# Up units of a squared-ReLU MLP as seven block products in place of eight

## The chip, the cores and the metric

The kernel runs on one core of a Trainium2 chip. The metric is the time of one execution in microseconds (us), as the device measures it. TensorE (PE) multiplies matrices into PSUM; VectorE (DVE), ScalarE (ACT) and GpSimd (POOL) work elementwise; SyncE (SP) issues transfers.

## What is computed

Two transformer blocks run one after the other on 512 tokens of 1024 features, in float32. The change touches the last piece of the second block:

```python
def sq_relu_mlp(h, w1, w2):
    return jnp.square(jax.nn.relu(h @ w1)) @ w2

    x = x + gt2[..., None, :] * sq_relu_mlp(modulate_2(rms_norm_2(x, norm2), sh2, sc2), w_mlp1, w_mlp2)
```

`w_mlp1` is 1024x4096 and `w_mlp2` is 4096x1024. Nothing else of the program is changed.

## The kernel before

**Data.** Features lie on the 128 partitions, tokens (T = 512) along the free axis; h is eight tiles of 128x512. Every float32 operand is split into a high part, rounded to the type fp32r, and the rest as a low part; `exact` and `products` multiply three times (high by high, high by low, low by high) and add up in PSUM.

**Units.** All weights come in units of 128x2048 floats (1 MB): 8 contraction tiles by 256 output features. A unit is loaded into `W_RAW[slot]` by SP, ScalarE casts it into `W_HI[slot]` (`split_hi`, L633), VectorE subtracts to get `W_LO[slot]` (`split_lo`, L1118), and TensorE does 8 tiles x 2 halves x 3 = 48 matmuls of 128x128 by 128x512 (L2059 to L2061). Slots alternate, so each unit is prepared while the one before it is multiplied. A unit fills two PSUM banks.

**The MLP.** It has four quarters, each of 4 up units and 4 out units: `quarter` at L571 (SP), L1086 (ACT), L1995 (DVE) and L2719 (PE). The first and the last are written out; the middle two are a hardware loop. For an up unit ScalarE applies ReLU to both banks (L1101), VectorE multiplies by the bank again, which is the square (L2010), casts to `G_HI` (L2020) and subtracts to `G_LO` (L2022). For an out unit VectorE adds both banks, gated, to the residual (`add_branch`, L1350).

**Order.** Each engine works its own queue in the order of the code. Semaphores order the engines: `landed` (a transfer), `hi_done` and `lo_done` (a unit split), `pe_done` (a unit multiplied), `evac_done` (its banks read), `relu_made`, `m_ready` (a tile of G ready for the out units). SP loads the next unit into a slot when the unit that held it has been split (`lo_done`).

Of the kernel before, what the change touches and what calls it, by code (L numbers as in the profile page):

```python
# [8 lines left out]
P = 128  # L9
# [177 lines left out]
def build(nc, ins, out):  # L187
    ctx_ = ExitStack()
    with ctx_:
        def sb(name, shape, dt=F32):  # L190
            return ctx_.enter_context(nc.sbuf_tensor(name, shape, dt))
# [133 lines left out]
        L_RAW = view("l_raw", 16, [P, KD, T])  # L325
        Y = view("merged", 0, [P, KD, T])
        SGB = [view(f"branch_gate{n}", 80 + 2 * n, [P, T]) for n in range(2)]
        STAT = sb("stat", [P, 64])

        PS = psum("ps", [P, 8 * T])  # L330
# [130 lines left out]
        def w_lo(u):  # L461


            return (W_RAW_LO if U_LR <= u.base < U_D + 2 else W_LO)[u.slot]

        block = ctx_.enter_context(nc.Block())

# [159 lines left out]
        def _(act):  # L627
# [455 lines left out]
            root(7)  # L1083
            h_hi(7, 7, U_MLP + 1)

            def quarter(q, last=False):  # L1086
                for j in range(4):
                    u = q.times(8) + (U_MLP + j)
                    if q.i is None and q.base == 0 and j == 0:
# [4 lines left out]
                    if not (q.i is None and q.base == 0 and j == 1):  # L1094
# [3 lines left out]
                    if q.i is None and q.base == 0 and j == 1:  # L1098
                        act.wait_ge(us_made, 3 * RAW.index(7) + 3)
                    for m in range(2):  # L1100
                        nc.scalar.activation(SA[m][:], BANK[2 * u.slot + m][:], ACT.Relu).then_inc(relu_made, 1)  # L1101
                for j in range(4):
                    if not (last and j == 3):
                        split_hi(q.times(8) + (U_MLP + 5 + j))

            quarter(at(0))
            with act.Fori(0, 2) as i:
                quarter(At(1, i, 1))
            quarter(at(3), True)
# [3 lines left out]
        def _(dve):  # L1113
# [878 lines left out]
            each(dve, 4, 0, 2, out_pair)  # L1992
            norm_split(7, 7, U_MLP + 1, (6, 7))

            def quarter(q, last_one=False):  # L1995
                for j in range(4):
                    u = q.times(8) + (U_MLP + j)
                    first = q.i is None and q.base == 0 and j == 0
                    if first:
                        raw_out(7)  # L2000
                    elif not (q.i is None and q.base == 0 and j == 1):
                        split_lo(u + 1)
                    for m in range(2):
                        t = 2 * j + m
                        n = q.times(8) + (t + 1)
                        dve.wait_ge(relu_made, n.v)
                        if first:
# [3 lines left out]
                        if first and m == 1:  # L2011
                            mul.then_inc(us_made, 1)
                            dve.wait_ge(us_made, 3 * RAW.index(7) + 3)
                        elif m == 1:
                            mul.then_inc(evac_done, 1)
                            dve.wait_ge(evac_done, (u + 1).v)
                        else:
                            mul.then_inc(y_a, 1)
                            dve.wait_ge(y_a, (q.times(4) + (KD + j + 1)).v)
                        nc.vector.tensor_copy(G_HI[:, t, :], GT[m][:]).then_inc(m_hi_made, 1)  # L2020
                        dve.wait_ge(m_hi_made, n.v)
                        nc.vector.tensor_tensor(G_LO[:, t, :], GT[m][:], G_HI[:, t, :].bitcast(F32), ALU.subtract).then_inc(m_ready, 1)  # L2022
                for j in range(4):
                    u = q.times(8) + (U_MLP + 4 + j)
                    if not (last_one and j == 3):
                        split_lo(u + 1)
                    dve.wait_ge(pe_done, (u + 1).v)
                    for m in range(2):
                        if last_one and j == 3 and m == 1:
                            last.then_inc(evac_done, 1)  # L2030
                            dve.wait_ge(pe_done, N_UNITS + 1)
                        last = add_branch(at(2 * j + m), BANK[2 * u.slot + m], 7)
                    last.then_inc(evac_done, 1)

            quarter(at(0))
            with dve.Fori(0, 2) as i:
                quarter(At(1, i, 1))
            quarter(at(3), True)
# [3 lines left out]
        def _(pe):  # L2042
# [676 lines left out]
            def quarter(q, count=4):  # L2719
                first = q.i is None and q.base == 0  # L2720
                for j in range(1 if first else 0, 4):
                    ready = (lambda k: pe.wait_ge(h_ready, H_BASE[7] + k + 1)) if first and j == 1 else None
                    products(q.times(8) + (U_MLP + j), KD, 2, h_part(H_HI), h_part(H_LO), ready).then_inc(pe_done, 1)
# [4 lines left out]
            quarter(at(0))  # L2728
            with pe.Fori(0, 2) as i:
                quarter(At(1, i, 1))  # L2730
            quarter(at(3), 3)
# [5 lines left out]
def weight_units(inputs):  # L2737


    w = {n: np.asarray(inputs[n]) for n in ("ffn_w_in", "ffn_w_out", "pool_w", "conv_w_in", "conv_w_out", "w_in_2",  # L2740
                                            "w_br_attn_2", "w_br_gla_2", "w_out_2", "w_mlp1_2", "w_mlp2_2")}
    units = np.zeros((N_UNITS, P, FULL), np.float32)

    def put(u, a, *cols):

        rows = np.concatenate([a[:, c:c + n].reshape(-1, P, n) for c, n in cols], axis=2).transpose(1, 0, 2)
        units[u, :, :rows[0].size] = rows.reshape(P, -1)

    for f in range(4):
        w_in, w_out = w["ffn_w_in"][f // 2, f % 2], w["ffn_w_out"][f // 2, f % 2]  # L2750
        for half in range(2):
            base = U_FFN[f] + half * (IN_UNITS + OUT_UNITS)
            for j in range(IN_UNITS):
                c = (half * FH + j) * P
                put(base + j, w_in, (c, P), (F + c, P))
            for m in range(OUT_UNITS):
                put(base + IN_UNITS + m, w_out[half * FH * P:(half + 1) * FH * P], (m * P, P))
    put(U_POOL, w["pool_w"][0].reshape(-1, 2 * P), (0, 2 * P))
    for j in range(8):
        put(U_CONV + j, w["conv_w_in"][0], (D + j * P, P), (2 * D + j * P, P))  # L2760
# [67 lines left out]
```

## Time and profile before

| | us |
|---|---|
| median of 3 runs | 2727.92 |
| lowest and highest | 2725.42, 2728.01 |
| the profiled execution | 2728.2 |
| its span, first to last instruction | 2726.1 |
| TensorE busy in the span | 2697.3 (99%) |
| VectorE busy | 1582.7 (58%) |
| ScalarE busy | 851.3 (31%) |

The mean granted TensorE clock is 0.997 of full speed. The span is 2.1 us shorter than the execution's own time. In the rows further down, a busy time of an instruction runs from its start to its end; two instructions of one engine can overlap by a little, so the distance from start to start is what an engine's queue costs.

### The profile page before, as it was taken

Reading aid. Unit: us, or ns where it says so; the run is one execution under the profiler, and the core shown is the slowest. Engines: PE = TensorE matmul, PEld = TensorE weight load, DVE = VectorE, ACT = ScalarE, POOL = GpSimd, SP = SyncE. Lnnn points to the kernel's source line nnn. Section 1 sums busy time; section 2 is a strip of 40 time slices with the busy share of each in tenths; the row PEclk is TensorE's granted clock in tenths of the full one; section 3 lists DMA queues with packets and bytes.
Section 4 is the critical chain, followed back from the end, with each engine's and each line's share of the span. In section 5 each row is a group of like instructions: output and inputs, shape, how many; then the busy total and the mean of one; then the engine's idle time right before and its main releaser. Section 6 shows DMA issues by size and latency. Waiting matters only on the chain.

```text
span 2726.1 us, 32568 instructions
## 1 busy us (share of the span) xinstructions
PE 2697.3 (99%) x12826; PEld 2255.3 (83%) x12826; DVE 1582.7 (58%) x2168; ACT 851.3 (31%) x956; POOL 74.2 (3%) x148
## 2 busy tenths in 40 slices
PE   7999999999999999999999999999999999999999
PEld 4888888888888888888888888899898888888887
DVE  6644658635576358554764445777687632654434
ACT  4212234222242122331421333345545512432221
POOL 0000000000001000000010000000000000000000
PEclk9999999999999999999999999999999999999999
DMA  7644523625526346222263332202212332222222
GB/s 289 233 144 168 203 100 124 226 106 187 180 103 240 130 156 223 100 100 101 92 243 119 131 109 95 102 36 68 69 53 66 128 135 92 93 93 94 94 106 77
DMA packets 61860, 355.05 MB, mean 130 GB/s; under 512 B 7104, under 2 KB 8896, under 8 KB 31680
## 3 DMA queue, kind: packets, MB, share of 16 engines
q1 hardware_dynamic: 42208, 252.20, 25.7%
q0 software_dynamic: 19120, 100.70, 10.5%
q8 instruction: 70, 1.15, 0.2%
q10 hardware_dynamic: 432, 0.75, 0.1%
q14 instruction: 30, 0.25, 0.0%
HBM read 343.66 MB, written 7.86 MB: 129 GB/s over the span
## 4 chain that ended last, share of the span: by engine, by line
PE 95%; DVE 3%; ACT 1%; issue 0%; DMA 0%; DVEq 0%; ACTq 0%
PE ps L2059 24%; PE ps L2060 24%; PE ps L2061 24%; PE ps L2279 5%; PE ps L2281 5%; PE ps L2280 5%; PE ps L2534 2%; PE ps L2479 1%; PE ps L2528 1%; PE ps L2079 1%; PE ps L2081 1%; PE ps L2080 1%; DVE h_lo L1257 0%; DVE w_lo L1118 0%; PE ps L2449 0%
## 5 line engine op out<-in xcount | busy, mean ns | idle before, releaser
L2059 PE MATMUL ps<-h_hi,w_hi 128*128 128x512 f32 x1888 | 736.4, 390 | 6.4 <-DVE g_t L1337 3.3
L2060 PE MATMUL ps<-h_lo,w_hi 128*128 128x512 f32 x1888 | 735.2, 389 | 0.0
L2061 PE MATMUL ps<-h_hi,w_lo 128*128 128x512 f32 x1888 | 735.1, 389 | 0.0
L633 ACT CAST w_hi<-w_raw 128x2048 fp32r<-128x2048 f32 (+1 forms) x238 | 419.3, 1762 | 598.6 <-PE ps L2061 517.9
L1118 DVE TENSOR_TENSOR w_lo<-w_raw,w_hi 128x2048 fp32r<-128x2048 f32 (+1 forms) x214 | 447.6, 2092 | 118.3 <-ACT w_hi L633 118.1
L2059 PEld LDWEIGHTS ps<-h_hi,w_hi 128*128 128x128 f32 x1888 | 354.7, 188 | 82.0 <-DVE g_t L1337 3.0
L2061 PEld LDWEIGHTS ps<-h_hi,w_lo 128*128 128x128 f32 x1888 | 354.9, 188 | 74.0
L2060 PEld LDWEIGHTS ps<-h_lo,w_hi 128*128 128x128 f32 x1888 | 354.9, 188 | 73.3
L2059 PE MATMUL ps<-g_hi,w_hi 128*128 128x512 f32 x944 | 367.3, 389 | 0.0
L2061 PE MATMUL ps<-g_hi,w_lo 128*128 128x512 f32 x944 | 367.2, 389 | 0.0
L2060 PE MATMUL ps<-g_lo,w_hi 128*128 128x512 f32 x944 | 367.2, 389 | 0.0
L1350 DVE SCALAR_TENSOR_TENSOR x_res<-ps,gate,x_res 128x512 f32<-128x512 f32 x120 | 87.6, 749 | 343.7 <-PE ps L2061 334.8
L722 ACT ACTIVATE silu_a<-ps 128x512 f32<-128x512 f32 x85 | 50.9, 599 | 638.9 <-PE ps L2061 633.8
L1373 DVE TENSOR_TENSOR g_t<-silu_a,ps 128x512 f32<-128x512 f32 x85 | 58.4, 687 | 301.4 <-ACT silu_a L722 301.4
L1133 DVE SCALAR_TENSOR_TENSOR ada<-ada,cond 128x1024 f32<-128x1024 f32 x176 | 207.9, 1220 | 1.6 <-DMA ada<-in_ada_t 1.5
L2061 PEld LDWEIGHTS ps<-g_hi,w_lo 128*128 128x128 f32 x944 | 177.2, 188 | 36.8
L2059 PEld LDWEIGHTS ps<-g_hi,w_hi 128*128 128x128 f32 x944 | 177.2, 188 | 36.7
L2060 PEld LDWEIGHTS ps<-g_lo,w_hi 128*128 128x128 f32 x944 | 177.2, 188 | 36.6
L2279 PE MATMUL ps<-h_hi,w_hi 128*128 128x512 f32 (+3 forms) x304 | 120.1, 395 | 0.5 <-DVE h_lo L1257 0.5
L2281 PE MATMUL ps<-h_hi,w_raw_lo 128*128 128x512 f32 (+3 forms) x304 | 113.5, 373 | 0.0
L2280 PE MATMUL ps<-h_lo,w_hi 128*128 128x512 f32 (+3 forms) x304 | 113.2, 372 | 0.0
L602 POOL DMA_DIRECT2D ada<-in_ada_t x64 | 33.8, 528 | 1359.2 <-DVE ada L1133 1356.6
(370 smaller groups left out, 3020.9 us busy)
## 6 DMA issues: line engine op xcount, KB each, us to landing
w_raw<-in_units SPq DMA_DIRECT2D x175, 1024.0 KB, 4.8
ada<-in_ada_t POOLq DMA_DIRECT2D x56, 1024.0 KB, 7.1
w_raw<-in_units SPq DMA_DIRECT2D x64, 704.0 KB, 4.0
ada<-in_ada_t POOLq DMA_DIRECT2D x64, 512.0 KB, 4.8
ada_first<-in_ada_t SPq DMA_DIRECT2D x8, 1024.0 KB, 12.1
x_res<-in_x SPq DMA_DIRECT2D x4, 512.0 KB, 7.8
x_home<-x_res POOLq DMA_DIRECT2D x1, 2048.0 KB, 8.3
attn_tq<-attn_qx SPq DMA_DIRECT2D x32, 64.0 KB, 2.0
```

Source lines behind the costliest of these rows:

```text
L633: nc.scalar.copy(W_HI[u.slot][:, 0:n], W_RAW[u.slot][:, 0:n]).then_inc(hi_done, 1)
L1118: nc.vector.tensor_tensor(w_lo(u)[:, 0:n], W_RAW[u.slot][:, 0:n], W_HI[u.slot][:, 0:n].bitcast(F32), ALU.subtract).then_inc(lo_done, 1)
L1133: return nc.vector.scalar_tensor_tensor(tile, tile, 1.0, COND[cond][:], ALU.mult, ALU.mult, accum_out=MOD_SUMS[:, bass.ds(n.v, 1)])
L1350: return nc.vector.scalar_tensor_tensor(x, bank[:], GATE[:, bass.ds((m + 8 * gate).v, 1)], x, ALU.mult, ALU.add)
L1373: nc.vector.tensor_tensor(GT[u.slot][:], SA[u.slot][:], bank[:], ALU.mult).then_inc(evac_done, 1)
L2059: pe.matmul(dst, hi[:, k, c], rhs_hi(k), start=(k == 0), stop=False)
L2060: pe.matmul(dst, hi[:, k, c], rhs_lo(k), start=False, stop=False)
L2061: last = pe.matmul(dst, lo[:, k, c], rhs_hi(k), start=False, stop=(k == kt - 1))
L2279: pe.matmul(dst, a_hi, b_hi, start=first, stop=False)
L2280: pe.matmul(dst, a_hi, b_lo, start=False, stop=False)
L2281: return pe.matmul(dst, a_lo, b_hi, start=False, stop=last)
L2534: last = pe.matmul(BANK[7][:, 2 * P:4 * P], VA[:, t, HD * (i // 2):HD * (i // 2 + 1)], PT[:, t, :, :].rearrange("p n q -> p (n q)"), start ...
```

## The change

The twelve up units of quarters 1 to 3 are computed by Strassen's product in Winograd's form. The 256 output features of a unit, its 1024 inputs and the 512 tokens are each halved, and the product is made from seven products of block sums in place of eight block products. In detail:

- The weights of such a unit lie in four quarters of 128x512 in DRAM (`put_quarters`). VectorE forms four sums of them (`w_sum_1` to `w_sum_4`); the seven left operands ("forms" 0 to 6) are three raw quarters, the third sum, which takes the place of a quarter, and three sum tiles. ScalarE casts each form to its high part and VectorE subtracts, form by form. Forms have fixed places in `W_HI` and `W_LO`, so form f of the next unit can be cast once product f of this unit is done.
- Once, during the out units of quarter 0, the block sums of h are made (`h_forms`, `h_forms_hi`): for each of 4 tiles six sums on VectorE, one cast on ScalarE, one 128x1024 subtraction on VectorE. They stay for all twelve units.
- TensorE does 7 products x 4 tiles x 3 = 84 matmuls of 128x128 by 128x256 a unit, into four banks, of which 256 columns each are used. Products 0 and 4 go to bank a, 2 and 5 to bank d, 3 and 6 to bank c, 1 to b. So product 4 waits for a copy of product 0 (`P_1`, ScalarE), product 5 for VectorE's second mixing step and product 6 for its third.
- VectorE puts the output together in seven additions of 128x256 (`mix` 0 to 5) into the SBUF tiles `C_1` and `C_2`. ScalarE does ReLU, the square and the cast to `G_HI` of each 128x512 tile (`squared`), and VectorE makes the eight `G_LO` tiles in the fourth up unit (`m_lo`).
- Quarter 0 and all out units keep their matmuls. The forms of a quarter's first up unit are made in the out unit before it.

The core of the diff, without 8 leading spaces (left out: semaphore names, tiles, `h_forms`, the renamed loops of quarter 0, `put_quarters`, and the deleted general `quarter`):

```diff
+def form_at(w, f):
+    return w[S0 if f < 4 else 1 - S0][:, (f % 4) * 4 * P:(f % 4 + 1) * 4 * P]
+def form_src(v, f):
+    return (raw_quarter(v, 0), S_2[:], raw_quarter(v, 2), S_1[:], raw_quarter(v, 1), raw_quarter(v, 3), S_4[:])[f]
+SUM_OF = {1: 3, 2: 2, 3: 1, 6: 4}
+def four(j):
+    return [BANK[4 * (j % 2) + n][:, 0:TC] for n in range(4)]
...
+    def form_hi_split(v, s, f, first=False):
+        if f == 0:
+            act.wait_ge(landed[v.slot], (v + 1).half().times(16).v)
+        elif f in SUM_OF:
+            act.wait_ge(sum_made, (s.times(4) + (SUM_MADE + SUM_OF[f])).v)
+        if first:
+            if f == 0:
+                act.wait_ge(pe_done, (v - 1).v)
+            if f == 4:
+                act.wait_ge(pe_done, v.v)
+        elif f < 6:
+            act.wait_ge(form_mm, (s.times(6) + (FORM_MM - 6 + f + 1)).v)
+        else:
+            act.wait_ge(pe_done, v.v)
+        nc.scalar.copy(form_at(W_HI, f), form_src(v, f)).then_inc(form_hi if f < 6 else hi_done, 1)
+    def whole_hi(v, s):
+        act.wait_ge(landed[v.slot], (v + 1).half().times(16).v)
+        for n in range(2):
+            act.wait_ge(form_mm, (s.times(6) + (FORM_MM + 2 * n + 2)).v)
+            c = slice(n * FULL // 2, (n + 1) * FULL // 2)
+            half = nc.scalar.copy(W_HI[v.slot][:, c], W_RAW[v.slot][:, c])
+        half.then_inc(hi_done, 1)
+    def squared(q, s, m, tile):
+        act.wait_ge(m_sq_made, (s.times(2) + (M_SQ + m - 1)).v)
+        nc.scalar.activation(SA[m][:], (C_2, C_1)[m][:], ACT.Relu).then_inc(relu_made, 1)
+        act.wait_ge(relu_made, (s.times(2) + (RELUS + m + 1)).v)
+        nc.scalar.activation(M_SQUARE[:, tile, :], SA[m][:], ACT.Square).then_inc(m_sq_made, 1)
+        act.wait_ge(m_sq_made, (s.times(2) + (M_SQ + m + 1)).v)
+        nc.scalar.copy(G_HI[:, tile, :], M_SQUARE[:, tile, :]).then_inc(m_hi_act, 1)
+    def mixed_unit(q, j):
+        u, s = q.times(8) + (U_MLP + j), sums_unit(q, j)
+        act.wait_ge(form_mm, (s.times(6) + (FORM_MM + 1)).v)
+        act.wait_ge(mix_made, (s.times(6) + (MIX_MADE - 1)).v)
+        nc.scalar.copy(P_1[:], four(j)[0]).then_inc(p1_made, 1)
+        if j < 3:
+            for f in range(6):
+                form_hi_split(u + 1, s + 1, f)
+        else:
+            whole_hi(u + 1, s)
+        act.wait_ge(mix_made, (s.times(6) + (MIX_MADE + 6)).v)
+        squared(q, s, 0, 2 * j)
+        if j < 3:
+            form_hi_split(u + 1, s + 1, 6)
+        act.wait_ge(evac_done, (u + 1).v)
+        squared(q, s, 1, 2 * j + 1)
...
+    def w_sum_1(v, s):
+        dve.wait_ge(landed[v.slot], (v + 1).half().times(16).v)
+        dve.wait_ge(form_lo, (s.times(6) + (FORM_LO - 2)).v)
+        nc.vector.tensor_tensor(S_1[:], raw_quarter(v, 2), raw_quarter(v, 3), ALU.add).then_inc(sum_made, 1)
+    def w_sum_3(v, s):
+        dve.wait_ge(sum_made, (s.times(4) + (SUM_MADE + 1)).v)
+        nc.vector.tensor_tensor(raw_quarter(v, 2), raw_quarter(v, 0), raw_quarter(v, 2), ALU.subtract).then_inc(sum_made, 1)
+    def w_sum_2(v, s):
+        dve.wait_ge(sum_made, (s.times(4) + (SUM_MADE + 1)).v)
+        nc.vector.tensor_tensor(S_2[:], S_1[:], raw_quarter(v, 0), ALU.subtract).then_inc(sum_made, 1)
+    def w_sum_4(v, s):
+        dve.wait_ge(sum_made, (s.times(4) + (SUM_MADE + 3)).v)
+        dve.wait_ge(lo_done, v.v)
+        nc.vector.tensor_tensor(S_4[:], raw_quarter(v, 1), S_2[:], ALU.subtract).then_inc(sum_made, 1)
+    def form_lo_split(v, s, f):
+        if f < 6:
+            dve.wait_ge(form_hi, (s.times(6) + (FORM_HI + f + 1)).v)
+        else:
+            dve.wait_ge(hi_done, (v + 1).v)
+        nc.vector.tensor_tensor(form_at(W_LO, f), form_src(v, f), form_at(W_HI, f).bitcast(F32),
+                                ALU.subtract).then_inc(form_lo if f < 6 else lo_done, 1)
+    def mix(q, j, n):
+        u, s = q.times(8) + (U_MLP + j), sums_unit(q, j)
+        a, b, d, c = four(j)
+        add = lambda out, x, bank: nc.vector.tensor_tensor(out, x, bank, ALU.add)
+        mixed = lambda n: dve.wait_ge(mix_made, (s.times(6) + (MIX_MADE + n)).v)
+        product = lambda f: dve.wait_ge(form_mm, (s.times(6) + (FORM_MM + f + 1)).v)
+        if n == 0:
+            dve.wait_ge(p1_made, (s + (P1_MADE + 1)).v)
+            mixed(0)
+            product(1)
+            add(U_2[:], P_1[:], b).then_inc(mix_made, 1)
+        if n == 1:
+            product(2)
+            mixed(1)
+            add(U_3[:], U_2[:], d).then_inc(mix_made, 1)
+        if n == 2:
+            product(3)
+            mixed(2)
+            dve.wait_ge(relu_made, (s.times(2) + (RELUS - 1)).v)
+            add(C_2[:, TC:T], U_3[:], c).then_inc(mix_made, 1)
+            dve.wait_ge(evac_done, u.v)
+            add(U_4[:], U_2[:], c).then_inc(mix_made, 1)
+        if n == 3:
+            product(4)
+            dve.wait_ge(relu_made, (s.times(2) + RELUS).v)
+            add(C_1[:, 0:TC], P_1[:], a).then_inc(mix_made, 1)
+        if n == 4:
+            product(5)
+            add(C_2[:, 0:TC], U_3[:], d).then_inc(mix_made, 1)
+        if n == 5:
+            dve.wait_ge(pe_done, (u + 1).v)
+            mixed(4)
+            add(C_1[:, TC:T], U_4[:], c).then_inc(evac_done, 1)
+    def m_lo(q, tile):
+        dve.wait_ge(m_hi_act, (q.times(8) + (M_HI_ACT - 8 + tile + 1)).v)
+        nc.vector.tensor_tensor(G_LO[:, tile, :], M_SQUARE[:, tile, :], G_HI[:, tile, :].bitcast(F32), ALU.subtract).then_inc(m_ready, 1)
+    def mixed_unit(q, j):
+        v, t = q.times(8) + (U_MLP + j + 1), sums_unit(q, j + 1)
+        if j == 3:
+            mix(q, j, 0)
+            mix(q, j, 1)
+            m_lo(q, 0)
+            m_lo(q, 1)
+            mix(q, j, 2)
+            m_lo(q, 2)
+            m_lo(q, 3)
+            split_lo(v)
+            mix(q, j, 3)
+            mix(q, j, 4)
+            m_lo(q, 4)
+            m_lo(q, 5)
+            mix(q, j, 5)
+            m_lo(q, 6)
+            m_lo(q, 7)
+            return
+        w_sum_1(v, t)
+        form_lo_split(v, t, 0)
+        w_sum_3(v, t)
+        w_sum_2(v, t)
+        mix(q, j, 0)
+        w_sum_4(v, t)
+        mix(q, j, 1)
+        form_lo_split(v, t, 1)
+        mix(q, j, 2)
+        form_lo_split(v, t, 2)
+        form_lo_split(v, t, 3)
+        mix(q, j, 3)
+        form_lo_split(v, t, 4)
+        mix(q, j, 4)
+        form_lo_split(v, t, 5)
+        mix(q, j, 5)
+        form_lo_split(v, t, 6)
...
+            elif not last_one:
+                if first:
+                    dve.wait_ge(t_ready, T_READY + 4)
+                w_sum_1(u + 1, q.times(4))
+                w_sum_3(u + 1, q.times(4))
+                w_sum_2(u + 1, q.times(4))
+                w_sum_4(u + 1, q.times(4))
+                for f in range(4):
+                    form_lo_split(u + 1, q.times(4), f)
...
+    def mixed_unit(q, j):
+        u, s = q.times(8) + (U_MLP + j), sums_unit(q, j)
+        a, b, d, c = four(j)
+        tokens = lambda hi, lo, k0, t0: lambda k: (hi[:, k0 + k, t0:t0 + TC], lo[:, k0 + k, t0:t0 + TC])
+        form = lambda n: lambda k: (T_HI[:, k, n * TC:(n + 1) * TC], T_LO[k // 2][:, k % 2, n * TC:(n + 1) * TC])
+        for f, dst, x in ((0, a, tokens(H_HI, H_LO, 0, 0)),
+                                 (1, b, form(1)),
+                                 (2, d, form(2)),
+                                 (3, c, form(0)),
+                                 (4, a, tokens(H_HI, H_LO, 4, 0)),
+                                 (5, d, form(3)),
+                                 (6, c, tokens(H_HI, H_LO, 4, TC))):
+            if f < 6:
+                pe.wait_ge(form_lo, (s.times(6) + (FORM_LO + f + 1)).v)
+            else:
+                pe.wait_ge(lo_done, (u + 1).v)
+            if f == 0:
+                pe.wait_ge(evac_done, (u - 1).v)
+            if f == 1:
+                pe.wait_ge(t_ready, T_READY + 4)
+            if f == 2 and j == 0:
+                pe.wait_ge(evac_done, u.v)
+            if f == 4:
+                pe.wait_ge(p1_made, (s + (P1_MADE + 1)).v)
+            if f == 5:
+                pe.wait_ge(mix_made, (s.times(6) + (MIX_MADE + 2)).v)
+            if f == 6:
+                pe.wait_ge(mix_made, (s.times(6) + (MIX_MADE + 4)).v)
+            hi, lo = form_at(W_HI, f), form_at(W_LO, f)
+            for k in range(4):
+                x_hi, x_lo = x(k)
+                cc = slice(k * P, (k + 1) * P)
+                last = exact(dst, hi[:, cc], lo[:, cc], x_hi, x_lo, k == 0, k == 3)
+            last.then_inc(form_mm if f < 6 else pe_done, 1)
```

## Rows read from the trace of the kernel before

**Rows 1.** The page, part 1 (busy time by engine) and part 4 (chain).

```profile
PE 2697.3 (99%) x12826; PEld 2255.3 (83%) x12826; DVE 1582.7 (58%) x2168; ACT 851.3 (31%) x956; POOL 74.2 (3%) x148
...
PE 95%; DVE 3%; ACT 1%; issue 0%; DMA 0%; DVEq 0%; ACTq 0%
```

**Rows 2.** Busy PE, PEld, DVE, ACT, POOL; PEclk; DMA share, GB/s: quarter 2, up, out.

```profile
2548.80:2592.30 43.50, 43.50 (x194) 36.03 (x193) 20.88 (x24) 10.58 (x10) 0.00 (x0) 1.00 0.26 96
2592.30:2635.80 43.50, 43.50 (x194) 36.03 (x193) 16.84 (x16) 8.63 (x6) 0.00 (x0) 1.00 0.28 97
```

**Rows 3.** TensorE in order of time: start, us, engine; 128x512 stream, 63 steps apart.

```profile
2500.40 0.39 PE L2059 MATMUL ps<-h_hi,w_hi 128*128 128x512 f32 x1
...
2514.68 0.39 PE L2059 MATMUL ps<-g_hi,w_hi 128*128 128x512 f32 x1
```

**Rows 4.** TensorE in order of time, 128x256 stream, 42 steps apart.

```profile
1738.40 0.28 PE L2279 MATMUL ps<-w_hi,h_hi 128*128 128x256 f32 x1
...
1743.44 0.28 PE L2279 MATMUL ps<-w_hi,h_hi 128*128 128x256 f32 x1
```

**Rows 5.** VectorE by line and shape: count | busy us, mean ns | idle before.

```profile
L1118 DVE TENSOR_TENSOR w_lo<-w_raw,w_hi 128x2048 fp32r<-128x2048 f32 x151 | 345.4, 2287 | 85.5 <-ACT w_hi L633 85.3 <-DVE conv_out L1546 0.2
```

**Rows 6.** VectorE in order of time, four places.

```profile
1720.14 0.42 DVE L1611 TENSOR_TENSOR low_rank<-ps,low_rank 32x256 fp32r<-32x256 f32 x1
1720.48 0.67 DVE L1613 TENSOR_TENSOR low_rank<-ps,low_rank 32x512 fp32r<-32x512 f32 x1
...
2172.16 4.90 DVE L1948 TENSOR_TENSOR l_lo<-l_raw,l_hi 128x512 fp32r<-128x512 f32 x8
...
2548.88 1.41 DVE L1350 SCALAR_TENSOR_TENSOR x_res<-ps,gate,x_res 128x512 f32<-128x512 f32 x2 [6.64 <-PE ps L2061]
...
2560.39 0.69 DVE L2010 TENSOR_TENSOR g_t<-silu_a,ps 128x512 f32<-128x512 f32 x1 [7.27 <-ACT silu_a L1101]
2561.11 0.43 DVE L2020 CAST g_hi<-g_t 128x512 fp32r<-128x512 f32 x1
```

**Rows 7.** ScalarE in order of time, three places.

```profile
23.26 0.72 ACT L770 ACTIVATE g_t<-g_t,mods 128x512 f32<-128x512 f32 x1 [4.49 <-DVE g_t L1449]
24.02 0.62 ACT L772 CAST h_hi<-g_t 128x512 fp32r<-128x512 f32 x1
...
2169.82 4.26 ACT L1053 CAST l_hi<-l_raw 128x512 fp32r<-128x512 f32 x8
...
2559.76 1.09 ACT L1101 ACTIVATE silu_a<-ps 128x512 f32<-128x512 f32 x2 [8.96 <-PE ps L2061]
2560.73 1.92 ACT L633 CAST w_hi<-w_raw 128x2048 fp32r<-128x2048 f32 x1
```

**Rows 8.** ScalarE by line and shape.

```profile
L646 ACT ACTIVATE g_t<-x_res 128x512 f32<-128x512 f32 x56 | 34.4, 624 | 52.9 <-DVE x_res L1350 29.3 <-DVE ssq L1186 14.4 <-DVE ssq L1190 9.2
...
L856 ACT CAST low_rank<-ps 96x256 fp32r<-96x256 f32 x1 | 0.4, 368 | 3.3 <-PE ps L2281 3.3
```

**Rows 9.** In order of time: VectorE ends, TensorE restarts.

```profile
2395.44 0.68 DVE L1337 TENSOR_TENSOR g_t<-ps,ssq 128x512 f32<-128x512 f32 x1
...
2396.27 0.47 PE L2059 MATMUL ps<-h_hi,w_hi 128*128 128x512 f32 x1 [1.12 <-DVE g_t L1337]
2396.58 0.40 PE L2060 MATMUL ps<-h_lo,w_hi 128*128 128x512 f32 x1
```

**Rows 10.** As rows 2, for two stretches; and two starts 12 steps apart.

```profile
1698.00:1700.00 2.00, 2.00 (x10) 2.00 (x11) 0.79 (x4) 0.21 (x1) 0.00 (x0) 0.50 0.04 8
...
2394.00:2396.00 2.00, 1.15 (x6) 0.61 (x4) 2.00 (x4) 0.00 (x0) 0.00 (x0) 1.00 0.00 0
...
1699.05 0.41 PE L2280 MATMUL ps<-h_lo,w_hi 128*128 128x256 f32 x1
...
1701.61 0.41 PE L2280 MATMUL ps<-h_lo,w_hi 128*128 128x256 f32 x1
```

**Rows 11.** The page, part 6: weight transfers, KB each, us to landing.

```profile
w_raw<-in_units SPq DMA_DIRECT2D x175, 1024.0 KB, 4.8
```

More of the change, by code:

```diff
@@ new lines, in outs, with first_quarter @@
+            def outs(q, last=False, first=False):
+                for j in range(4):
+                    if j < 3:
+                        split_hi(q.times(8) + (U_MLP + 5 + j))
+                    elif not last:
+                        for f in range(7):
+                            form_hi_split(q.times(8) + (U_MLP + 8), q.times(4), f, True)
+                    if first:
+                        for kk in ((0,), (1, 2), (3,), ())[j]:
+                            h_forms_hi(kk)
+            def first_quarter():
+                for j in range(4):
+                    u = at(U_MLP + j)
+                    if j == 0:
@@ L1093, in quarter @@
                         continue
-                    if not (q.i is None and q.base == 0 and j == 1):
+                    if j > 1:
                         split_hi(u + 1)
@@ L1101, in quarter @@
                         nc.scalar.activation(SA[m][:], BANK[2 * u.slot + m][:], ACT.Relu).then_inc(relu_made, 1)
+                outs(at(0), first=True)
+            def quarter(q, last=False):
                 for j in range(4):
-                    if not (last and j == 3):
-                        split_hi(q.times(8) + (U_MLP + 5 + j))
-            quarter(at(0))
+                    mixed_unit(q, j)
+                outs(q, last)
+            first_quarter()
             with act.Fori(0, 2) as i:
@@ L2000, in quarter, with first_quarter @@
+            def first_quarter():
+                for j in range(4):
+                    u = at(U_MLP + j)
+                    if j == 0:
                         raw_out(7)
-                    elif not (q.i is None and q.base == 0 and j == 1):
+                    elif j > 1:
                         split_lo(u + 1)
@@ L2018, in quarter @@
                             mul.then_inc(y_a, 1)
-                            dve.wait_ge(y_a, (q.times(4) + (KD + j + 1)).v)
+                            dve.wait_ge(y_a, KD + j + 1)
                         nc.vector.tensor_copy(G_HI[:, t, :], GT[m][:]).then_inc(m_hi_made, 1)
-                        dve.wait_ge(m_hi_made, n.v)
+                        dve.wait_ge(m_hi_made, t + 1)
                         nc.vector.tensor_tensor(G_LO[:, t, :], GT[m][:], G_HI[:, t, :].bitcast(F32), ALU.subtract).then_inc(m_ready, 1)
+                outs(at(0), first=True)
+            def quarter(q, last_one=False):
                 for j in range(4):
[L2024 to L2035, printed above, removed]
+                    mixed_unit(q, j)
+                outs(q, last_one)
+            first_quarter()
             with dve.Fori(0, 2) as i:
@@ L2717, in last_unit @@
                     last.then_inc(pe_done, 1)
[L2719 to L2723, printed above, removed]
+            def mixed_unit(q, j):
[12 more added lines that the diff above has]
+                        pe.wait_ge(form_lo, (s.times(6) + (FORM_LO + f + 1)).v)
+                    else:
+                        pe.wait_ge(lo_done, (u + 1).v)
[17 more added lines that the diff above has]
+                    last.then_inc(form_mm if f < 6 else pe_done, 1)
@@ L2747, in put, with put_quarters @@
         units[u, :, :rows[0].size] = rows.reshape(P, -1)
+    def put_quarters(u, a, *cols):
+        blocks = [a[4 * P * half:4 * P * (half + 1), c:c + P].reshape(4, P, P).transpose(1, 0, 2).reshape(P, 4 * P)
+                  for c in cols for half in range(2)]
+        units[u] = np.concatenate(blocks, axis=1)
     for f in range(4):
```

102 lines of the change are left out of this document (89 added, 13 removed).

## The prediction

> **What bounds the kernel now.** I read the busy times first [rows 1]: TensorE is busy 99% of the span and carries 95% of the chain that ended last, VectorE is busy 58%, ScalarE 31%. Then the stretches of one quarter of the MLP [rows 2]: TensorE is busy all of the 43.5 us of its up units and all of its out units, VectorE 20.9 and 16.8 us, ScalarE 10.6 and 8.6. So here nothing but TensorE's stream counts. Its pace has to be taken from starts, not from durations, since a matmul of 0.39 us overlaps the next: 63 steps in 14.28 us are 0.2267 us for 512 columns [rows 3], 48 of them 10.88 us a unit. A stream of 256 columns is in the trace too: 42 steps in 5.04 us, 0.120 us each [rows 4], each with a weight load of its own, as in the new code.
>
> **TensorE's share of the change.** 84 x 0.120 = 10.08 us in place of 10.88: 0.80 us less for each of twelve units, 9.6 us at most. It is less than an eighth, because 256 columns cost 0.53 of 512.
>
> The Trainium skill, in "TensorE: Matmul & The Clock Gate" (Back-to-back issue gap), has isolated matmuls start every N / 2.4 + 2.5 ns; by that a unit would go from 10.36 to 9.17 us and the most to be had would be 14 us. The trace has 0.2267 and 0.120 where the rule gives 0.216 and 0.109, so the rows decide.
>
> **What the other two engines get.** Prices from start to start. VectorE: a 128x512 subtraction 0.60 (8 in 4.90, the last one lasting 0.69), 128x256 0.34, the next instruction when it needs the result of the one before 0.03 after its end [rows 6]; the two additions to the residual 1.32 together [rows 6]; a whole split 2.29 [rows 5]. ScalarE: a 128x512 cast from SBUF 0.52 (8 in 4.26), lasting 0.62, the next dependent one 0.04 after the end [rows 7]; the square of 128x512 lasts 0.62 as well, and the 256 columns from PSUM 0.37, so 0.28 in a queue [rows 8]. From ScalarE's end to VectorE's start 0.03 [rows 6, 7].
>
> For one of the first three up units VectorE has 4 sums and 7 subtractions of 512 columns and 7 additions of 256: 11 x 0.60 + 7 x 0.34 = 9.0 us. ScalarE has 7 casts, 6 steps of `squared` and the copy of product 0: about 8.1 us with the dependent steps. Both fit into 10.08 taken alone. They don't fit together, because the two queues wait for each other in a ring that closes once a unit:
>
> - ScalarE, from the end of `mix` 4 (both halves of `C_2`): handover 0.04, ReLU 0.66, square 0.66, cast 0.52, the cast of form 6 0.52, the second `squared` 1.83, `P_1` 0.28, the cast of form 0 for the unit after next 0.62 and 0.03: 5.15 us.
> - VectorE, from there: the subtraction of form 0 stands near the front of the next unit's queue, and behind it come `w_sum_3`, `w_sum_2`, `mix` 0, `w_sum_4`, `mix` 1, form 1, `mix` 2 (two), forms 2 and 3, `mix` 3, form 4, `mix` 4: 8 x 0.60 + 5 x 0.34 + 0.43 = 6.93 us.
>
> Sum 12.08 us a turn, whatever TensorE does. TensorE hangs on it at product 5, which needs `mix` 1 (bank d read); `mix` 1 ends 3.77 us before `mix` 4.
>
> **A quarter, clock at TensorE's first product of its first up unit.** Forms 0 to 3 are ready.
>
> Unit 0: VectorE does the residual additions from 0.20 to 1.52, forms 4 to 6 to 3.33, then its queue without a pause, `mix` 1 ending at 7.1, before product 5 is due (7.20), and `mix` 4 at 10.86. No stall; the unit ends at 10.08.
>
> Unit 1: one turn on, `mix` 4 ends at 22.94 and `mix` 1 at 19.17. Product 5 was due at 17.28. TensorE restarts 0.15 after VectorE's end and its first step is 0.08 longer than 0.23 [rows 9]: 19.40, a stall of 2.1 us. Products 5 and 6 take 2.88: 22.28.
>
> Unit 2: `mix` 1 ends at 31.25, product 5 starts at 31.48 where 29.48 was due: 2.0 us. Unit end 34.36.
>
> Unit 3: VectorE has no forms to make. `P_1` is copied at 39.24, `mix` 1 ends at 40.5, product 5 is due at 41.5: no stall; end 44.44. But VectorE's queue goes on with `m_lo` 0 and 1 (1.2), `mix` 2 (0.68), `m_lo` 2 and 3 (1.2), and only then the split of the first out unit, 43.5 to 45.8. The out unit starts at 46.0: a stall of 1.6 us.
>
> Out units: 4 x 10.88 to 89.55, where 8 x 10.88 = 87.04 stood before. Their VectorE work (four sums, seven subtractions, 6.6 us more in the last) fits beside 16.8 of 43.5 us [rows 2].
>
> So 3.2 us gained and 5.7 lost: 2.5 us more a quarter, 7.5 in three. From the profiled execution's 2728.2 that is 2735.7; its time and the median of 2727.9 differ by 0.3, and I forecast 2736.
>
> **The rest.** The sums of h in quarter 0 cost VectorE about 5.3 us a tile (two additions and a cast waited for, four of 256 columns, 1.2 for the subtraction, half a split's price): 21 us, with its other work some 41 of the 43.5 us of out units. The crowded place is the second out unit, 14 us of work in 10.88; the banks it reads late are wanted one unit on, and by my queue VectorE catches up 2.6 us before the quarter ends. Cost nothing; if that cover is gone, the overrun. Weight transfers are as many and land after 4.8 us [rows 11]; a unit is issued when its slot's forms are split, 4 us into a unit at worst, and wanted no sooner than a unit later. SP and GpSimd queues are untouched otherwise. ReLU from SBUF isn't in the trace: between 0.60 and the 0.72 of an activation with a bias [rows 7, 8]; I take the square's 0.62. Up to four such steps lie in a turn, so -0.1 to +0.4 us. The new code waits more, often two or three times before a 0.34 us addition, on values worked out in the loop. ScalarE passes two such waits without a gap within 0.47 us [rows 7], so one costs between nothing and 0.24 us, hidden as long as the instruction before is running. Unseen, I take nothing; behind blocking waits it could add up to 1 us a turn.
>
> **Rivals.**
>
> *TensorE stays the bound.* If ScalarE and VectorE overlapped better than the queue order allows, each unit would take 10.08: 2728.2 - 9.6 = 2718.6. It decides if the turn is under 10.1 us, 2 us less than my sum. For it: both engines' plain sums are under 10.08. Against: every price in the ring is a row. 0.07.
>
> *The ring holds, the closing stall doesn't.* If the split in unit 3 came 1.6 us earlier, a quarter would cost +0.9: 2731, within what can be told from no change. 0.13.
>
> *Waits lengthen the ring.* With 1 us more a turn, units 1 and 2 and what follows shift: 2 to 2.5 us a quarter, 2742 to 2743; with two, 2749. 0.17.
>
> *The clock falls.* At 1698 to 1700 the granted clock was 0.50, half of 2.4 GHz, after a run of one-column products, and a 256-column step took 0.213 us (12 in 2.56) [rows 10]; at 2394 to 2396, with a gap of 1.1 us, it stayed at 1.00. My stalls are 2 us, longer than any in these rows. Four microseconds at the half clock lose 1.8; after the first two stalls the ring hides it, ahead of the out units about 0.3 to 2.2 a quarter isn't: 2737 to 2742, I take 2740. 0.05. The Trainium skill, in "TensorE: Matmul & The Clock Gate" (What's actually happening), gates the clock to half after an idle window; by that rule this rival would win only if a stall grows beyond those I expect, and no row shows a 2 us gap.
>
> *It doesn't do what it says,* 256-column steps paced by the weight load (0.19): excluded by rows 4.
>
> **How the numbers follow.** My forecast has 0.58, own range 2731 to 2741. A measurement of this kernel tells about 0.2% (5.5 us) from no change, so "slower" begins at 2733.4. Faster 0.08 (first rival, rounded up); same 0.18 (second rival, and 0.05 of mine); slower 0.74. The range takes in the second rival and most of the third and fourth: 2729 to 2746.
>
> **What would show it.** In the profile after: 256-column steps of 0.120; in quarters 1 to 3 up units of 10.1, 12.1, 12.1 and 10.1 us, with TensorE idle about 2 us before product 5, put down to VectorE's `mix` 1; the first out unit waiting 1.6 us for `w_lo`; VectorE waiting for the cast of form 0, ScalarE for `mix` 4; clock 1.00. Units 1 and 2 of 10.1 us make the ring wrong; 13 us and more, or gaps before each short addition, the cost of waits; a stall in quarter 0, the cover for the sums of h.

## The result, and the profile after

The changed kernel takes 2735.69 us, median of 6 runs (2732.01 to 2736.21), beside 2727.76 us (6 runs, 2723.74 to 2728.15) for the kernel before: a ratio of 1.0029, 95% interval 1.0016 to 1.0042. On a second chip (10 and 15 runs) it was 2732.9 beside 2725.38, 1.0026 (1.0017 to 1.0035). So it is slower by 7.5 to 7.9 us, though TensorE has less to do. The forecast was 2736, slower by 7.5.

The page of the changed kernel, part 1, where [rows 1] had 2697.3 us on TensorE, 1582.7 on VectorE and 851.3 on ScalarE. The profiled execution took 2732.01 us, its span 2730.2:

```profile
PE 2690.3 (99%) x13258; PEld 2269.0 (83%) x13258; DVE 1654.6 (61%) x2352; ACT 914.3 (33%) x1095; POOL 74.3 (3%) x148
```

TensorE is busy 7 us less in a span that is 4 us longer. Now one quarter, the third as in [rows 2], split where its first out unit starts (from, to; us; busy PE, PEld, DVE, ACT, POOL; granted clock; DMA share, GB/s):

```profile
2547.60:2593.60 46.00, 41.02 (x337) 40.41 (x335) 36.71 (x69) 27.18 (x48) 0.00 (x0) 1.00 0.26 91
2593.60:2637.10 43.50, 43.47 (x192) 36.02 (x193) 19.58 (x24) 11.61 (x13) 0.00 (x0) 1.00 0.27 96
```

The up units take 46.0 us in place of 43.5 and TensorE idles 5 of them, at full clock. VectorE has 36.7 us of work in 46 and ScalarE 27.2: neither is full. TensorE in order of time shows where it idles (start, us, engine, line; in brackets the idle time and who ended it):

```profile
2547.59 0.28 PE L2550 MATMUL ps<-h_hi,w_hi 128*128 128x256 f32 x1
...
2564.84 0.28 PE L2552 MATMUL ps<-h_hi,w_lo 128*128 128x256 f32 x1
2566.97 0.36 PE L2550 MATMUL ps<-h_forms_hi,w_hi 128*128 128x256 f32 x1 [1.85 <-DVE mix L2171]
...
2577.00 0.28 PE L2552 MATMUL ps<-h_hi,w_lo 128*128 128x256 f32 x1
2579.04 0.36 PE L2550 MATMUL ps<-h_forms_hi,w_hi 128*128 128x256 f32 x1 [1.76 <-DVE mix L2171]
...
2591.95 0.28 PE L2552 MATMUL ps<-h_hi,w_lo 128*128 128x256 f32 x1
2593.63 0.49 PE L2330 MATMUL ps<-g_hi,w_hi 128*128 128x512 f32 x1 [1.40 <-DVE w_lo L1238]
...
2637.28 0.28 PE L2550 MATMUL ps<-h_hi,w_hi 128*128 128x256 f32 x1
```

Three gaps and no other: before product 5 of units 1 and 2, waiting for `mix`, and ahead of the first out unit, waiting for the split of its weights. In the quarter's own clock product 5 starts at 19.38 and 31.45, the out unit at 46.04, the next quarter at 89.69.

The ring, one turn of it. First ScalarE, then VectorE, in order of time:

```profile
2558.52 0.63 ACT L1168 ACTIVATE silu_a<-mixed 128x512 f32<-128x512 f32 x1 [1.38 <-DVE mixed L2171]
...
2560.90 0.63 ACT L1168 ACTIVATE silu_a<-mixed 128x512 f32<-128x512 f32 x1
...
2562.75 0.36 ACT L1179 COPY prod<-ps 128x256 f32<-128x256 f32 x1
2563.01 0.62 ACT L1149 CAST w_hi<-w_raw 128x512 fp32r<-128x512 f32 x1
...
2570.59 0.63 ACT L1168 ACTIVATE silu_a<-mixed 128x512 f32<-128x512 f32 x1 [1.29 <-DVE mixed L2171]
```

```profile
2557.99 0.41 DVE L2171 TENSOR_TENSOR mixed<-mix,ps 128x256 f32<-128x256 f32 x1
...
2561.02 0.69 DVE L2164 TENSOR_TENSOR w_lo<-w_sum,w_hi 128x512 fp32r<-128x512 f32 x1 [1.68 <-ACT w_hi L1149]
2561.63 0.69 DVE L2143 TENSOR_TENSOR w_sum<-w_raw 128x512 f32<-128x512 f32 x1
2563.67 0.69 DVE L2164 TENSOR_TENSOR w_lo<-w_raw,w_hi 128x512 fp32r<-128x512 f32 x1 [1.35 <-ACT w_hi L1149]
...
2566.41 0.41 DVE L2171 TENSOR_TENSOR mix<-mix,ps 128x256 f32<-128x256 f32 x1
...
2570.15 0.41 DVE L2171 TENSOR_TENSOR mixed<-mix,ps 128x256 f32<-128x256 f32 x1
```

`mix` 4 at 2557.99 lets ScalarE begin the squares of unit 0. The cast of form 0 stands behind both squares and `P_1` in ScalarE's queue and starts at 2563.01. VectorE waits for it 1.35 us, goes on without a pause from 2563.67, and reaches `mix` 1 (which frees product 5) at 2566.41 and the next `mix` 4 at 2570.15. Then ScalarE is released again. A turn is 12.16 us; TensorE's unit is 10.08.

All waits from the first of these quarters to the end, summed (us in total, times, longest), four of them:

```profile
ACT silu_a L1168 <- DVE mixed L2171: 25.1, 12, 5.1
DVE w_lo L2164 <- ACT w_hi L1149: 21.6, 15, 1.7
...
PE ps L2550 <- DVE mix L2171: 9.3, 6, 1.9
...
PE ps L2330 <- DVE w_lo L1238: 2.7, 2, 1.4
```

Six waits for `mix`, so the ring is there in every quarter, and two for the split: in the first of the three quarters a lower clock had slowed TensorE just before (see the last section), and of that stall 0.39 us from start to start was left, too little to be listed. From here on a "quarter" is the time from one first product to the next; for the last one, where no quarter follows, it is the time to the span's end less the 3.39 us that the kernel before has there (90.43 - 87.04, spans unrounded). The changed kernel has 89.89, 89.69 and 89.54 where 87.04 stood, 8.0 us together.

### The profile page after: what moved, and what is told of

The parts are those of the page before. It is cut to its first block and busy times, and to the rows that moved or that the text cites. A ratio compares the mean times of both kernels' runs of the same rounds, so it can differ in the third digit from the quotient of the medians.

```text
span 2730.2 us, 34144 instructions
## 1 busy us (share of the span) xinstructions
PE 2690.3 (99%) x13258; PEld 2269.0 (83%) x13258; DVE 1654.6 (61%) x2352; ACT 914.3 (33%) x1095; POOL 74.3 (3%) x148
## 5 line engine op out<-in xcount | busy, mean ns | idle before, releaser
L2330 PE MATMUL ps<-h_hi,w_hi 128*128 128x512 f32 x1696 | 661.7, 390 | 6.4 <-DVE g_t L1457 3.3
L2331 PE MATMUL ps<-h_lo,w_hi 128*128 128x512 f32 x1696 | 660.4, 389 | 0.0
L2332 PE MATMUL ps<-h_hi,w_lo 128*128 128x512 f32 x1696 | 660.4, 389 | 0.0
L681 ACT CAST w_hi<-w_raw 128x2048 fp32r<-128x2048 f32 (+1 forms) x223 | 390.6, 1751 | 520.4 <-PE ps L2332 438.7
L2330 PEld LDWEIGHTS ps<-h_hi,w_hi 128*128 128x128 f32 x1696 | 318.8, 188 | 74.4 <-DVE g_t L1457 3.0
L2332 PEld LDWEIGHTS ps<-h_hi,w_lo 128*128 128x128 f32 x1696 | 318.8, 188 | 66.3
L2331 PEld LDWEIGHTS ps<-h_lo,w_hi 128*128 128x128 f32 x1696 | 318.8, 188 | 66.0
L2332 PEld LDWEIGHTS ps<-g_hi,w_lo 128*128 128x128 f32 x944 | 177.2, 188 | 36.7
L2550 PE MATMUL ps<-h_hi,w_hi 128*128 128x512 f32 (+3 forms) x448 | 161.1, 360 | 0.5 <-DVE h_lo L1377 0.5
L2551 PE MATMUL ps<-h_lo,w_hi 128*128 128x512 f32 (+3 forms) x448 | 154.3, 344 | 0.0
L2550 PEld LDWEIGHTS ps<-h_hi,w_hi 128*128 128x128 f32 (+1 forms) x448 | 85.8, 191 | 12.7 <-issue 1.4
```

The lines of the kernel that those rows point to most:

```text
L681: nc.scalar.copy(W_HI[u.slot][:, 0:n], W_RAW[u.slot][:, 0:n]).then_inc(hi_done, 1)
L2330: pe.matmul(dst, hi[:, k, c], rhs_hi(k), start=(k == 0), stop=False)
L2331: pe.matmul(dst, hi[:, k, c], rhs_lo(k), start=False, stop=False)
L2332: last = pe.matmul(dst, lo[:, k, c], rhs_hi(k), start=False, stop=(k == kt - 1))
L2550: pe.matmul(dst, a_hi, b_hi, start=first, stop=False)
L2551: pe.matmul(dst, a_hi, b_lo, start=False, stop=False)
```

## Experiments

Each edit is shown against the changed kernel. The theory is the ring: what matters is only what stands between `mix` 4 and the cast of form 0 on ScalarE, and VectorE's queue from there. The rivals are that ScalarE or VectorE is simply short of time (the sum of its work), and that short instructions with several waits cost something of their own.

**The split sooner.** VectorE, in the last up unit, splits the out unit's weights ahead of the four subtractions for the squares.

```diff
-                    m_lo(q, 0)
-                    m_lo(q, 1)
                     mix(q, j, 2)
-                    m_lo(q, 2)
-                    m_lo(q, 3)
                     split_lo(v)
+                    for tile in range(4):
+                        m_lo(q, tile)
```

> One part of the VectorE order moved: in the fourth up unit of a quarter the split of the first out unit stands right behind mix 2 (and mix 2 ahead of the m_lo tiles), not behind four m_lo. Theory (the stall at the head of the out units is the queue position of the split): the split ends at about 43.7 of the quarter's clock, before TensorE is through with the unit at 44.4, so that stall (1.4 to 1.6 us) is gone, 3 to 5 us in three quarters: 2731 to 2733 against 2735.7. The two stalls ahead of product 5 stay at 2 us each. Rival (VectorE has too much work in the up units, wherever it stands): no change.

Measured: 2730.14 us (10 runs) beside 2724.81 (20 runs), 1.0019 (1.0009 to 1.0028). Two quarters of 88.20, where 89.69 stood. In the second of them the two gaps before product 5 stay at 2.13 and 2.05 from start to start; in the first the clock fell after the first gap, and the second one shrank to 0.56. The closing gap is gone, on TensorE:

```profile
2591.38 0.28 PE L2550 MATMUL ps<-h_hi,w_lo 128*128 128x256 f32 x1
2591.57 0.50 PE L2328 MATMUL ps<-g_hi,w_hi 128*128 128x512 f32 x1
```

So the closing stall is VectorE's queue order, worth 1.5 us a quarter, and independent of the ring. The last quarter, though, took 89.50; why is told below, with the clock. That leaves 3.2 us for the three quarters in the trace. The times alone hardly show it: 1.0019 stands beside 1.0026 and 1.0029, and the intervals overlap.

**The squares late.** ScalarE alone is reordered: the squares of unit u are made in unit u+1, the first behind the cast of form 0, the second behind that of form 3. The work is the same.

```diff
                 nc.scalar.copy(P_1[:], four(j)[0]).then_inc(p1_made, 1)
-                if j < 3:
-                    for f in range(6):
+                    form_hi_split(u + 1, s + 1, 0)
+                if j > 0:
+                    square_of(j - 1, 0)
+                if j < 3:
+                    for f in range(1, 4):
                         form_hi_split(u + 1, s + 1, f)
...
-                squared(q, s, 0, 2 * j)
+                if j > 0:
+                    square_of(j - 1, 1)
                 if j < 3:
-                    form_hi_split(u + 1, s + 1, 6)
-                act.wait_ge(evac_done, (u + 1).v)
-                squared(q, s, 1, 2 * j + 1)
+                    for f in range(4, 7):
+                        form_hi_split(u + 1, s + 1, f)
+                else:
+                    square_of(3, 0)
+                    square_of(3, 1)
```

> Only ScalarE's order changed: the two squares of an up unit are made in the unit after it, the first behind the cast of form 0, the second behind the cast of form 3. Same instructions on every engine. Theory (a ring of ScalarE and VectorE through mix 4, the squares, P_1 and form 0): the ring is opened, VectorE's 9.0 us and ScalarE's 8.1 us a unit fit under TensorE's 10.08, the stalls ahead of product 5 go, at most 0.3 us is left at the head of the out units: a quarter of 84.1 us in place of 89.8, 17 us less in three, 2719. Rival (one of the two engines is full): no change, or under 2 us.

Measured: 2716.11 us (5 runs) beside 2724.81, 0.9968 (0.9954 to 0.9982), 0.3% faster than the kernel before. Quarters 84.35, 84.33 and 84.25. No gap before product 5 is left; ScalarE, in the unit that had the ring:

```profile
2554.50 0.62 ACT L1149 CAST w_hi<-w_raw 128x512 fp32r<-128x512 f32 x1
2555.02 0.63 ACT L1168 ACTIVATE silu_a<-mixed 128x512 f32<-128x512 f32 x1
```

The cast of form 0 now stands ahead of the ReLU, and the ReLU no longer waits, since its `mixed` is long made. The same instructions on the same engines, in another order, are worth 5.4 us a quarter. That excludes both sums of work as the cause of the loss, and the waits themselves, which are all still there.

**Only the second square late.** The second square of a unit is made behind `P_1` and the cast of form 0 of the next unit; the first stays.

```diff
+                def second(jj):
+                    act.wait_ge(evac_done, (q.times(8) + (U_MLP + jj + 1)).v)
+                    squared(q, sums_unit(q, jj), 1, 2 * jj + 1)
+
                 if j < 3:
-                    for f in range(6):
+                    form_hi_split(u + 1, s + 1, 0)
+                if j > 0:
+                    second(j - 1)
+                if j < 3:
+                    for f in range(1, 6):
                         form_hi_split(u + 1, s + 1, f)
...
-                act.wait_ge(evac_done, (u + 1).v)
-                squared(q, s, 1, 2 * j + 1)
+                else:
+                    second(3)
```

> Only the second square of a unit moves, behind P_1 and the cast of form 0 of the next unit. Theory: the ring gets shorter by exactly the 1.83 us of one square, 12.1 to 10.3 us a turn, so the stalls ahead of product 5 fall from 2.0 to 0.2 or 0.3 us, not to zero; with about 0.5 us left at the head of the out units a quarter takes 84.8 us, 2721. Rival (stalls come from another wait that the order of the squares touches only by the way): stalls that aren't 1.8 us shorter.

Measured: 2722.01 us (8 runs) beside 2724.81, 0.9986 (0.9975 to 0.9996); quarters 85.51, 85.51 and 85.35. The direction holds, the size does not: 0.7 us above what was expected. VectorE shows why:

```profile
2554.99 0.41 DVE L2180 TENSOR_TENSOR mixed<-mix,ps 128x256 f32<-128x256 f32 x1
...
2558.02 0.69 DVE L2173 TENSOR_TENSOR w_lo<-w_sum,w_hi 128x512 fp32r<-128x512 f32 x1 [1.68 <-ACT w_hi L1149]
...
2565.70 0.41 DVE L2180 TENSOR_TENSOR mixed<-mix,ps 128x256 f32<-128x256 f32 x1
```

A second ring lay under the first. It closes through the cast of form 6, which still stands behind the first square: 2.62 us from `mix` 4's end to VectorE's start on form 6, then 8.09 us of VectorE to the next `mix` 4, its queue now with form 6, `w_sum_1` and form 0 ahead. Sum 10.71 (product 5 starts 10.62 apart, at 2562.54 and 2573.16), still above 10.08, and 1.45 below the first ring rather than the 1.83 that the square takes.

**Each square twice.** ScalarE takes the square of every tile twice, first into a tile that nobody reads.

```diff
+                nc.scalar.activation(GT[m][:], SA[m][:], ACT.Square)
                 nc.scalar.activation(M_SQUARE[:, tile, :], SA[m][:], ACT.Square).then_inc(m_sq_made, 1)
```

> The order of the changed kernel, but ScalarE makes each square twice, once into an unused tile: 0.53 us more for each of two tiles a unit. ScalarE's sum goes from 8.1 to 9.2 us, still under TensorE's 10.08. Theory: the work lies in the ring, 12.1 to 13.2 us a turn, and adds up over the three turns of a quarter: about 3.2 us a quarter, 9.5 in all, 2745. Rival (only the sum of an engine's work counts): no change.

Measured: 2741.59 us (4 runs) beside 2724.81, 1.0058 (1.0041 to 1.0075); quarters 92.83, 92.83 and 92.67, 2.9 to 3.1 above the changed kernel. Product 5 now starts every 13.11 us (2478.60, 2491.71) where 12.07 stood: 1.04 more, and two squares of 0.54 from start to start are 1.08. The gap, on TensorE:

```profile
2569.03 0.28 PE L2553 MATMUL ps<-h_hi,w_lo 128*128 128x256 f32 x1
2571.43 0.35 PE L2551 MATMUL ps<-h_forms_hi,w_hi 128*128 128x256 f32 x1 [2.12 <-DVE mix L2172]
```

What ScalarE gets in the ring comes out at the end, nearly one for one. A second, smaller gap is new: product 4 starts 0.80 after the matmul before it (at 2567.62), since `P_1` now comes late as well; it lies within the 13.11.

**The changed kernel again,** on the chip of the next two.

> The changed kernel once more, on the same chip as the two that follow, so that they stand against it as well as against the kernel before. Every theory expects quarters of 89.7 to 89.9 us on TensorE's clock and a time 7.5 to 8 us above the kernel before: 2732 to 2736, ratio 1.003.

Measured: 2732.9 us (10 runs) beside 2725.38 (15 runs); quarters 89.87, 89.70 and 89.54.

**Squares late and split sooner.** Both edits together.

> Two edits together: ScalarE makes the squares of unit u in unit u+1, behind the first and the third further cast there, and VectorE splits the first out unit's weights before the four subtractions for the squares of unit 3. If the loss was the ring of ScalarE and VectorE and the queue order ahead of the first out unit, nothing but TensorE's stream is left: 4 x 10.08 + 4 x 10.88 = 83.84, with the restarts of a stream some 84.0 to 84.1 a quarter (the squares alone moved gave 84.34, with a gap of 0.27 ahead of the out units). The time is then 2715 to 2716 beside 2716 for the squares alone: ratio 0.996 to the kernel before, and 16 to 20 us under the changed kernel. If the added units cost something of their own beyond the ring (short instructions that wait, memory shared by the engines), the quarter stays above 84.3.

Measured: 2715.69 us (5 runs) beside 2725.38, 0.9961 (0.9947 to 0.9974); 17.2 us under the changed kernel on the same chip, 9.7 under the kernel before. Quarters 83.98, 83.98 and 84.06. Windows as above, and TensorE in order of time:

```profile
2542.50:2582.90 40.40, 40.40 (x337) 40.34 (x336) 34.98 (x66) 27.60 (x48) 0.00 (x0) 1.00 0.29 104
2582.90:2626.50 43.60, 43.60 (x195) 36.09 (x194) 21.37 (x27) 11.61 (x13) 0.00 (x0) 1.00 0.27 96
```

```profile
2542.50 0.28 PE L2563 MATMUL ps<-h_hi,w_hi 128*128 128x256 f32 x1
...
2582.79 0.28 PE L2565 MATMUL ps<-h_hi,w_lo 128*128 128x256 f32 x1
2582.91 0.41 PE L2343 MATMUL ps<-g_hi,w_hi 128*128 128x512 f32 x1
```

TensorE is busy all of 84 us; four up units take 40.41. This is the change with its own gain alone: 3.06, 3.06 and 2.98, together 9.1 us of the 9.6 that the two step times (0.2267 and 0.120) allow.

**The same, each square twice.**

> The version with the squares moved and the split sooner, and in it each of the two squares of a unit is taken twice, the second time into a tile that nobody reads: the same 2 x 0.6 us more on ScalarE a unit that cost the changed kernel 3.0 us a quarter. By the ring theory they now lie outside the ring, and ScalarE has about 8 + 1.3 us of work in a unit of 10.08: 0 to 0.3 us a quarter, 2715 to 2717. By the rival that ScalarE's sum of work, or the traffic of its extra instructions, set the time, it is again about 3 us a quarter: 2724 to 2725.

Measured: 2717.68 us (5 runs) beside 2725.38, 0.9967 (0.9954 to 0.9980); quarters 84.59, 84.58 and 84.58, 0.5 to 0.6 more than without, where the same instructions cost 2.9 to 3.1 inside the ring. That is above the 0 to 0.3 expected. Nearly all of it is one gap, before the second out unit. ScalarE, VectorE and TensorE in order of time:

```profile
2506.24 1.91 ACT L681 CAST w_hi<-w_raw 128x2048 fp32r<-128x2048 f32 x1
```

```profile
2508.18 2.29 DVE L1254 TENSOR_TENSOR w_lo<-w_raw,w_hi 128x2048 fp32r<-128x2048 f32 x1 [1.12 <-ACT w_hi L681]
```

```profile
2509.83 0.39 PE L2346 MATMUL ps<-g_hi,w_lo 128*128 128x512 f32 x1
2510.53 0.50 PE L2344 MATMUL ps<-g_hi,w_hi 128*128 128x512 f32 x1 [0.31 <-DVE w_lo L1254]
```

In the last up unit both pairs of squares run in a row, and the cast of the second out unit's weights stands behind them; doubled, they push it past its slack (in the profile without the doubling the same split ends at 2509.23, and TensorE comes to that unit at 2509.82). It costs by a queue's order once more, not by a sum. The up units keep their 40.41 us.

Every edit to the ring was on ScalarE's side. That VectorE's queue makes up the rest of a turn is read from its rows, where it works 6.89 and 8.09 us without a pause; no run makes that queue shorter or longer within the ring.

## Why the prediction was right

**TensorE's step.** 84 steps were put at 10.08 us. With the squares late and the split sooner, three of the four up units take 10.08 and the first 10.17. That 0.09 is most of the 0.14 by which the quarter exceeds 83.84: in the first unit `mix` 1 ends at 7.08 of the quarter's clock, and with 0.15 for the restart product 5 starts at 7.23, where 7.20 was due. The prediction had `mix` 1 at 7.1 and called it no stall; it left its own 0.15 out there. The other 0.05 lies in the out units.

**The ring.** ScalarE's part was put at 5.15 us (its terms add up to 5.16) and is 5.27 (from `mix` 4's end at 2558.40 to form 0 at 2563.67): the handover to the waiting ReLU was put at 0.04 from an engine that hardly waited [rows 7] and is 0.12. VectorE's part was 6.93 and is 6.89. The turn, 12.08, is 12.16 in this quarter and 12.07 between the starts of product 5. The ReLU from SBUF, 0.62 by the square, lasts 0.63. The waits of the new code, taken at nothing, cost nothing: VectorE runs the eleven instructions from 2563.67 to `mix` 3 at 2569.21 in 5.54 us, seven of 0.60 and four of 0.33.

**The stalls.** Product 5 at 19.40 and 31.48 in the quarter's clock: 19.38 and 31.45. The first out unit at 46.0: 46.04. The quarter 89.55: 89.69, of which 0.10 is the out unit's restart, whose first step takes 0.33 and not 0.23, a term that was counted before product 5 and left out here. Quarter 1 has 0.2 more, by the clock.

**What was costed at nothing.** The sums of h in quarter 0 were hidden: from TensorE's restart among its up units (2396.27 before [rows 9], 2392.32 after) to the next quarter's first product it takes 65.38 us where 65.37 stood, and VectorE idles 2.90 us ahead of the residual additions (2.6 predicted). The transfers landed in time; no wait names them.

**The total.** Three quarters at +2.5 made 7.5; they make 8.0 in the trace, 7.9 and 7.5 in the two comparisons of medians. That 2736 lies 0.3 from the median of 2735.69 is partly luck: single executions of this kernel took 2732.0 to 2736.2, and its median on the second chip is 2732.9. The difference is the better test.

**The rivals.** TensorE as the bound (0.07) needed a turn under 10.1: it was 12.1; with the squares moved and the split sooner TensorE is the bound again, at 9.1 us gained in place of 9.6. The closing stall gone (0.13) is what the first experiment made, by an edit. Longer waits (0.17): no. The clock (0.05) is half right: it did fall, see below, but in the changed kernel the ring hid most of it. The prediction's ground for its low chance was that none of its rows showed a gap of 2 us. The trace of before has one, elsewhere in the program, and the clock fell behind it (last section): the chance of 0.05 rested on too few rows.

## What to carry to other kernels

When work moves from the full engine to two idle ones, a sum of busy time is not enough: follow both queues around until they close, and compare that turn with the bound's step. An instruction whose result is wanted late (here the squares, read only by the out units) must not stand in a queue ahead of one that closes the ring; and under the longest ring there can be a next one, as here at 10.7 us under 12.1, where an edit's gain ends.

## What the hardware showed

**Gaps of 1.8 us sometimes halve the clock.** After the first gap of the last quarter of the changed kernel (windows as above):

```profile
2656.00:2658.00 2.00, 1.42 (x10) 1.45 (x11) 2.00 (x6) 1.38 (x3) 0.00 (x0) 0.89 0.00 0
2658.00:2660.00 2.00, 2.00 (x12) 2.00 (x11) 2.00 (x5) 0.62 (x1) 0.00 (x0) 0.50 0.00 0
```

The granted clock is 0.50, 1.2 GHz, and a 256-column step takes 0.213 us. In the four profiles with gaps (the changed kernel twice, the split sooner, each square twice) this followed 8 of the 19 gaps of 1.75 us idle or more ahead of product 5; in those without such gaps it never came in the MLP. After a first gap it cost the changed kernel nothing: its next gap shrank to 0.28 us idle. After a second gap it cost that kernel 0.2 us (the first of its three quarters, 89.89), since the stall ahead of the out units shrank with it. With the split sooner it came after the second gap of the last quarter, where nothing downstream idles any more:

```profile
2666.00:2668.00 2.00, 1.40 (x9) 1.44 (x10) 2.00 (x6) 1.40 (x3) 0.00 (x0) 0.79 0.00 0
2668.00:2670.00 2.00, 2.00 (x11) 2.00 (x11) 2.00 (x5) 0.62 (x1) 0.00 (x0) 0.50 0.00 0
```

That is the 89.50 of that quarter against 88.20 of the two others: 1.3 us.

The trace of before could have told. At 67.60 TensorE restarts after 2.25 us idle, in a stream of 512 columns, and the clock falls:

```profile
67.60 0.50 PE L2059 MATMUL ps<-h_hi,w_hi 128*128 128x512 f32 x1 [2.25 <-DVE g_t L1373]
...
68.00:70.00 2.00, 2.00 (x7) 1.59 (x6) 1.90 (x5) 1.85 (x1) 0.00 (x0) 0.59 0.85 295
```

The same gap is in all nine profiles, and in seven of them the clock fell behind it.

The Trainium skill, in "TensorE: Matmul & The Clock Gate" (What's actually happening), gates the clock after an idle window that runs free of the kernel. The prediction took from it that a stall longer than 2 us would be needed; the rows, with 1.75 to 2.25 us, say otherwise, and they decide. That some gaps of one length are followed by a fall and others aren't would fit a window that runs free, but no run here moved a gap against such a window.

**An unchanged stretch that varies by 3 us.** Both kernels' times come in two groups some 3.5 us apart (of the first runs, 2732.0 and 2733.0 beside 2735.6 to 2736.2). Ahead of the MLP, after the run of one-column products [rows 10], the kernel before has this:

```profile
1695.00:1700.00 5.00, 5.00 (x31) 5.00 (x32) 1.61 (x5) 1.34 (x3) 0.00 (x0) 0.65 0.54 183
1700.00:1705.00 5.00, 5.00 (x23) 3.96 (x23) 2.29 (x4) 0.48 (x1) 0.00 (x0) 0.67 0.05 17
```

and the changed kernel this:

```profile
1695.00:1700.00 5.00, 5.00 (x39) 4.52 (x39) 2.06 (x6) 0.50 (x3) 0.00 (x0) 1.00 0.40 140
1700.00:1705.00 5.00, 4.54 (x22) 3.06 (x21) 4.87 (x8) 2.83 (x4) 0.00 (x0) 1.00 0.00 0
```

From the first of those products (1694.15 and 1693.31) to the next stream of h with 512 columns (1706.08 and 1702.10) it takes 11.93 us with the fall and 8.79 without. So the profiled execution of before carries 3.1 us that the one of after doesn't; another 0.8 was there ahead of this stretch. That is why their spans differ by 4.1 while the quarters differ by 8.0. It doesn't explain the two groups by itself: the profiled executions of the split sooner and of the second square late had this fall too (11.65 and 11.76 us), and their times, 2729.92 and 2720.65, are in the lower group of their kernel; but those two are the ones whose clock did not fall after the gap at 67 us. What makes the groups stays open, since the timed executions left no such rows. A difference of a few us between single executions of this kernel is to be read from the quarters.
